# Key rows of a cached window turned in 32 by 32 blocks on VectorE, with query columns spread by key quarter

## The chip, the core and the metric

The kernel runs on one core of a Trainium2 chip. The metric is the device time of one execution in microseconds (us); where several executions are given, their median counts. TensorE multiplies, VectorE, ScalarE and GpSimd (POOL) work on the two on-chip memories SBUF and PSUM, and SyncE (SP) issues most of the transfers. Each engine runs its own instructions in order and waits on semaphores for the others.

## The reference, cut to what matters

One layer of a decoder: attention and a short gated convolution side by side, one output projection, then a mixture of experts and a gated input embedding. There are 1024 new prompt positions and 8 sample batches of 4 new tokens. The part that the change touches is the samples' attention: each batch has 2048 cached key and value rows of 8 heads by 64, and its 4 tokens see three dilation patterns of them and the batch's own new tokens.

```
DILATED_PATTERNS = ((128, 1), (512, 4), (2048, 16))
s = einsum('bthc,btkhc->bthk', q, kg) * HEAD_DIM ** -0.5 + bias
s = where(valid, s, NEG)
p = softmax(s, axis=-1)
out = einsum('bthk,btkhc->bthc', p, vg)
```

The convolution group computes `B * conv3(C * h)` over 512 channels for all tokens.

## The kernel before

The stages follow each other: projections of q, k and v for all tokens, attention of the prompt (32 steps), then a **convolution stage** that also does the whole sample attention, then the output projection, routing, the experts and the embedding. The last three hold most of the time and are not touched.

The convolution stage makes 12 groups (`NCONV`) of 7 products (`PRODUCTS`), each four f32 matmuls of 128 x 128 by 264 columns; the seven are a fast scheme for a 2 x 2 block product. I call each of these 84 products with what hangs behind it a **slot**. The product of a slot goes to one of three PSUM banks in turn. ScalarE copies the first four of a group (`keep_product`), VectorE adds the seven together in "joins" (`join_product`), multiplies the gates (`use_first`, `use_second`) and makes the three taps of the convolution (`taps`), and POOL prepares sums of the next group's weights. A product may start when its bank has been read.

The sample attention is cut into parts (`SAMPLE_PARTS`), and `spread_parts` gives each part a slot in proportion to its `ROOM`. In its slot every engine does its own share of the part, after the product or its joins: on VectorE, before, ahead of the taps. The parts of batch b:

- ("key", b, gg), gg = 0 to 3: the 896 cached rows that the patterns need (512 near, 384 far) lie in a ring slot `KV` of three. For two heads (128 columns) TensorE turns the seven 128 x 128 blocks (`keys`, L2816 and L2820), and ScalarE copies the two banks to `near` and `far` (L1387, L1391).
- ("score", b): TensorE multiplies the keys with the query columns `qbd`, for 512, 384 and 32 (new) columns, four heads' pairs at a time on four strips of the array (`score_keys`, L2837). Four batches share one score bank pair.
- "soft", "norm" and ("turn", g) follow once for each **pass** g of four batches: VectorE adds the bias and finds the maximum (L2077), ScalarE takes the exponential, VectorE divides (L2082), TensorE turns the weights in eight blocks (`turn_ps`) and ScalarE copies them to `PTs`.
- ("weigh", b) multiplies the weights with the values (`weigh_values`), VectorE masks the result by head (L2090), and ("sum", b) adds the rows that belong together (L2877).

SP loads the ring: four transfers per item, when the item three places earlier has been used up; between them stand the loads of the convolution's weights, in the order of their slots. At the start SP also loads small tables, among them eight transfers of the bias table into `relbd` (L707), ahead of the first saves of turned rows (`keep_xT`, L717).

## Time and profile before

| what | value |
| --- | --- |
| median of 3 runs | 1082.56 us (1079.72 to 1084.94) |
| the profiled execution | 1082.67 us |
| its span, first to last instruction | 1080.7 us |
| granted TensorE clock, mean | 0.982 of full speed |
| TensorE busy | 1036.0 us, 96% |
| VectorE busy | 523.0 us, 48% |
| ScalarE busy | 312.7 us, 29% |
| convolution stage | 280.13 to 498.25 us |

A busy share is an average over stages. The profile can also be cut into windows, into groups of instructions by line, or listed in order of time; beside an instruction it says how long its engine idled before it and what ended that. Times of single instructions overlap a little at their ends.

### The profile page before, as it was taken

The page shows a single profiled execution, that of the slowest core. Times are in us where ns is not written, and L with a number is a line of the kernel's source. Part 1 is how long each engine was busy: PE and PEld are TensorE (multiplying, and loading weights), DVE is VectorE, ACT ScalarE, POOL GpSimd, SP SyncE. Part 2 cuts the span into 40 slices and gives each one's busy share as a digit, 9 for nine tenths or more (in the row PEclk, how much of TensorE's full clock was granted, in tenths as well). Part 3 has the DMA queues.
Part 4 walks back from the last instruction along what each step waited for, and adds up shares of the span by engine and source line. Part 5 has one row for each costly group of instructions (what it writes and reads, how often), then busy time and mean ns, then how long its engine had stood idle before and what let it go on. Part 6 is the DMA issues. An engine that isn't in the chain of part 4 may idle for free.

```text
span 1080.7 us, 15684 instructions
## 1 busy us (share of the span) xinstructions
PE 1036.0 (96%) x5834; PEld 620.1 (57%) x5834; DVE 523.0 (48%) x1175; ACT 312.7 (29%) x665; POOL 212.4 (20%) x240
## 2 busy tenths in 40 slices
PE   7999999999999999999999999989999999889997
PEld 6888875565878777766555554334433333345443
DVE  6836634777733464545556464441111110047674
ACT  2332313777533322301111123111111111244331
POOL 0100001121433352531012111322231110130000
PEclk9999999999999999999999998989999999989999
DMA  9713214940563666663973237989999999974321
GB/s 315 190 31 116 71 50 119 293 101 6 215 213 112 212 211 216 207 244 81 355 270 128 94 105 280 405 340 414 418 410 410 419 420 399 371 288 157 119 78 78
DMA packets 99260, 242.11 MB, mean 224 GB/s; under 512 B 21206, under 2 KB 56958, under 8 KB 84528
## 3 DMA queue, kind: packets, MB, share of 16 engines
q1 hardware_dynamic: 88544, 212.10, 54.1%
q0 software_dynamic: 9920, 26.38, 6.4%
q10 hardware_dynamic: 720, 2.62, 0.6%
q8 instruction: 48, 0.79, 0.3%
q14 instruction: 28, 0.23, 0.1%
HBM read 210.12 MB, written 35.65 MB: 227 GB/s over the span
## 4 chain that ended last, share of the span: by engine, by line
PE 80%; DVE 6%; DMA 6%; SPq 4%; issue 2%; ACT 2%; POOL 0%; POOLq 0%; DVEq 0%; ACTq 0%
PE pair L2921 13%; PE pair L3124 13%; PE pair L2598 10%; PE pair L2976 9%; PE pair L3146 6%; PE pair L3228 5%; PE pair L3223 3%; PE pair L2739 2%; DMA h_dram<-R 2%; DMA R<-in_w_up 2%; PE pair L2713 2%; PE pair L3047 2%; PE pair L2755 2%; PE pair L3111 1%; SPq L707 1%
## 5 line engine op out<-in xcount | busy, mean ns | idle before, releaser
L2921 PE MATMUL pair<-R 128*128 128x264 f32 x672 | 160.2, 389 | 0.2 <-POOL R L1032 0.2
L3124 PE MATMUL pair<-R 128*32 128x512 f32 (+2 forms) x896 | 151.3, 601 | 5.2 <-DMA R<-in_w_up 3.0
L2598 PE MATMUL pair<-R 128*128 128x256 f32 x672 | 149.7, 382 | 0.4 <-DVE R L1755 0.4
L2598 PEld LDWEIGHTS pair<-R 128*128 128x128 f32 x672 | 127.0, 191 | 18.8 <-issue 1.0
L2921 PEld LDWEIGHTS pair<-R 128*128 128x128 f32 x672 | 123.5, 190 | 23.4 <-issue 3.5
L2976 PE MATMUL pair<-R 128*128 128x512 f32 x256 | 116.6, 606 | 0.0
L2329 DVE TENSOR_TENSOR R<-pair,R 128x256 f32<-128x256 f32 x21 | 8.9, 425 | 208.3 <-ACT R L1516 208.3
L3124 PEld LDWEIGHTS pair<-R 128*32 128x32 f32 (+2 forms) x896 | 48.8, 125 | 92.2 <-issue 87.8
L3146 PE MATMUL pair<-R,bias 128*32 128x512 f32 (+2 forms) x448 | 78.0, 611 | 2.7 <-issue 2.1
L2976 PEld LDWEIGHTS pair<-R 128*128 128x128 f32 x256 | 47.7, 192 | 53.3 <-issue 52.6
L3228 PE MATMUL pair<-R 128*128 128x512 f32 x168 | 73.0, 593 | 0.0
L1031 POOL TENSOR_TENSOR R<-R 128x256 f32<-128x256 f32 x48 | 38.2, 796 | 115.8 <-DMA R<-in_w_in 113.6
L1953 DVE TENSOR_TENSOR R<-R 128x264 f32<-128x264 f32 x48 | 29.7, 619 | 56.2 <-ACT R L1371 55.2
L3228 PEld LDWEIGHTS pair<-R 128*128 128x128 f32 x168 | 31.5, 190 | 38.2 <-issue 38.2
L1371 ACT ACTIVATE R<-pair 128x264 f32<-128x264 f32 x48 | 18.8, 391 | 107.7 <-PE pair L2921 107.7
L1516 ACT ACTIVATE R<-pair 128x256 f32<-128x256 f32 x21 | 8.1, 384 | 137.5 <-PE pair L3124 137.5
L3146 PEld LDWEIGHTS pair<-R,bias 128*32 128x32 f32 (+2 forms) x448 | 23.4, 125 | 41.9 <-issue 39.5
L1127 POOL DMA_INDIRECT R<-m_dram,lists x21 | 21.3, 1013 | 122.9 <-PE pair L3111 87.9
L1767 DVE TENSOR_TENSOR R<-pair,R 128x256 f32<-128x256 f32 x48 | 20.3, 422 | 44.2 <-PE pair L2598 43.8
L1888 DVE CUSTOM_DVE_ANT_0 R<-pair,R 128x384 f32<-128x384 f32 (+6 forms) x64 | 32.4, 544 | 16.2 <-issue 15.7
L1032 POOL TENSOR_TENSOR R<-R 128x256 f32<-128x256 f32 x48 | 40.2, 838 | 0.0
L1135 POOL DMA_INDIRECT y_dram<-R,lists x21 | 21.0, 1002 | 97.6 <-ACT R L1528 94.3
(366 smaller groups left out, 1471.5 us busy)
## 6 DMA issues: line engine op xcount, KB each, us to landing
R<-in_w_gate SPq DMA_DIRECT2D x32, 1024.0 KB, 12.3
R<-in_w_up SPq DMA_DIRECT2D x32, 1024.0 KB, 15.6
R<-in_w_down SPq DMA_DIRECT2D x32, 1024.0 KB, 16.8
R<-in_w_in SPq DMA_DIRECT2D x12, 1024.0 KB, 8.4
R<-in_x_prompt SPq DMA_DIRECT2D x16, 512.0 KB, 3.8
R<-in_cache_k SPq DMA_DIRECT2D x8, 1024.0 KB, 5.0
R<-in_cache_v SPq DMA_DIRECT2D x8, 1024.0 KB, 4.9
R<-y_dram SPq DMA_DIRECT2D x16, 512.0 KB, 5.9
```

What stands on the lines that cost most here:

```text
L1031: pool.tensor_tensor(out[:, 0:2, :], x[:, 0:2, :], y[:, 0:2, :], op)
L1032: return pool.tensor_tensor(out[:, 2:4, :], x[:, 2:4, :], y[:, 2:4, :], op)
L1888: dve.tensor_tensor_reduce(E[n % 3][hh][:, lo:hi], bk[2 * (n % 2) + hh][:, lo:hi], Z[s][:, at + lo:at + hi], -1.0, 3e38, ALU.add, ALU.min, ...
L1953: dve.tensor_tensor(out, x, y, op).then_inc(S("cv_join"), 1)
L2598: last = mm(qbank(p, part, k), lhs[:, c, :], rhs[:, c, :], start=(c == 0), stop=(c == 3))
L2713: last = mm(dst[hh][:, near_lo:hi], QT[halves_[hh], pair, P * i:P * i + P], KT[halves_[hh], pair, k0:P * i + P], start=True, stop=True)
L2921: last = mm(cbank(n, k), lhs[:, c, :], rhs[:, c, :], start=(c == 0), stop=(c == 3))
L2976: last = mm(bk[2 * pair + j][0:n, :], lhs[:, q, P * a.t:P * a.t + P], w_out[:, c0 + q, 512 * j:512 * j + 512], start=(q == 0), stop=(q == ...
L3124: last = mm(bk[2 + u][r, :].rearrange("p (w f) -> p w f", w=2), xgT[u][:, c, r], wgu[s][:, :, c, :], start=(c == 0), stop=(c == DC - 1))
L3146: last = mm(bk[4 + j][r, :], hT[u][:, q, r], wd[s][:, q, 512 * j:512 * j + 512], start=(q == 0), stop=(q == 1))
L3223: last = mm(bk[2 + j], hnT[i][:, c, :], w_pg[c][:, 512 * j:512 * j + 512], start=(c == 0), stop=(c == DC - 1))
L3228: last = mm(pbank(p, nth), x[:, c, :], w[:, c, :], start=(c == 0), stop=(c == 3))
```

## The change

**Keys.** TensorE no longer turns the keys. A key's near rows are loaded so that the 32 partitions of quarter i hold the rows of one residue (four transfers instead of one; the far rows three as before), and VectorE turns a ring slot's rows in blocks of 32 x 32 straight into `kT` (two instructions per key part, `turn_keys`). Within a partition quarter there now lies a quarter of the rows (224) for 32 of a head's 64 channels. So a batch's scores are 16 matmuls of 256 columns (224 cached, 32 new), and the query columns are spread such that each key quarter meets its own copy (`spread_q`, with masks `in_strip`).

**Passes.** A pass is two batches instead of four (`NPASS` = 4). A row of scores now belongs to one key quarter, so the minimum and the sum over a head's four quarters are taken with small block turns (`by_group`). The weights' turn is four matmuls against a permuted identity, four times instead of twice, and six ScalarE copies behind each.

**Order.** `SAMPLE_PARTS` is written by `sample_order`; soft and norm have places of their own; the ring's items alternate between keys and values earlier. In a slot VectorE now does the taps ahead of the sample part.

**Elsewhere.** The sample's q and k are turned by 32 small matmuls (`trans_qk`) in place of eight turns, and VectorE copies q to `q4` in 16 copies inside the attention steps 9 to 24. The eight loads of `relbd` have a quarter of their former elements and stand behind the first two `keep_xT`; VectorE completes the table with one copy. The bias is added by quarter.

```diff
-SAMPLE_PARTS = (("key", 0, 0), ("key", 0, 1), ("key", 0, 2), ("key", 0, 3), ("score", 0),
...
-ROOM = {"key": 4, "score": 4, "turn": 6, "weigh": 8, "sum": 4}
+def sample_order():
+    parts = []
+    for g in range(NPASS + 1):
+        keys = [[("key", 2 * g + d, gg) for gg in range(NG)] if g < NPASS else [] for d in range(2)]
+        if g == 0:
+            parts += keys[0] + [("score", 0)] + keys[1] + [("score", 1), ("soft", 0)]
+            continue
+        b = 2 * g - 2
+        parts += [*keys[0][0:1], ("norm", g - 1), *keys[0][1:2], ("turn", g - 1), *keys[0][2:4]]
+        if g < NPASS:
+            parts += [("score", 2 * g)]
+        parts += [("weigh", b), *keys[1][0:2], ("sum", b), ("weigh", b + 1), *keys[1][2:4]]
+        if g < NPASS:
+            parts += [("score", 2 * g + 1), ("soft", g)]
+        parts += [("sum", b + 1)]
+    return parts
+ROOM = {"key": 4, "score": 6, "soft": 2, "norm": 2, "turn": 4, "weigh": 8, "sum": 4}
...
+        def turn_keys(b, gg):
+            slot, arrived = item("k", b)
+            kv = KV[slot]
+            if gg == 0:
+                dve.wait_ge(S(f"ring_in{slot}"), arrived)
+                if b >= 1:
+                    dve.wait_ge(S("ss_done"), b)
+                else:
+                    dve.wait_ge(S("ssa_full"), 1)
+            raw = kv[:, :, P * gg:P * gg + P].rearrange("p c (n x) -> p c n x", n=4)
+            out = kT[:, 4 * gg:4 * gg + 4, 0:PART].rearrange("p n (c r) -> p c n r", c=7)
+            dve.transpose(out[:, 0:4], raw[:, 0:4])
+            dve.transpose(out[:, 4:7], raw[:, 4:7]).then_inc(S("kt_done"), 1)
...
         def score_sample(g):
-            dve.wait_ge(S("ss_done"), 4 * g + 4)
-            if g == 1:
-                dve.wait_ge(S("st_full"), 3)
-            dve.tensor_tensor_reduce(Es, bank[3][:, 0:SKN], bias_s[:, :], -1.0, 3e38, ALU.add, ALU.min, nms).then_inc(S("ss_scored"), 1)
+            dve.wait_ge(S("ss_done"), 2 * g + 2)
+            if g >= 1:
+                dve.wait_ge(S("st_full"), g)
+            for s in range(2):
+                then(dve.tensor_tensor_reduce(Es[:, s, :], bk[6 + g % 2][:, ROW * s:ROW * s + ROW], bias_s, -1.0, 3e38, ALU.add, ALU.min,
+                                              least[:, s:s + 1]))
+                if 2 * g + s + 1 < NB:
+                    new_bias(2 * g + s + 1)
+            by_group(least_t, ALU.min, least, group_least, nms).then_inc(S("ss_scored"), 1)
+            for b in (2 * g + 2, 2 * g + 3):
+                if b < NB:
+                    spread_q(b)
...
         def normalise_sample(g):
-            dve.wait_ge(S("ss_exp"), g + 1)
-            then(dve.reciprocal(rdens, dens))
-            dve.tensor_scalar(Es, Es, rdens, None, ALU.mult).then_inc(S("ps_ready"), 1)
+            dve.wait_ge(S("ss_exp"), 2 * g + 2)
+            then(by_group(dens_t, ALU.add, dens, group_den, rdens))
+            for s in range(2):
+                dve.tensor_scalar(Es[:, s, :], Es[:, s, :], rdens[:, s:s + 1], None, ALU.mult).then_inc(S("ps_ready"), 1)
...
+                if n >= 1 and k < 3:
+                    taps(n - 1, k)
                 for part in PARTS_AT.get(at, ()):
                     sample_part(*part)
-                if n >= 1 and k < 3:
-                    taps(n - 1, k)
...
         def score_keys(b):
-            for c0, c1, rhs in ((0, NEAR, near), (NEAR, SK, far), (SK, SKN, kts)):
-                for gg in range(NG):
-                    last = mm(bank[3][strips[gg], c0:c1], qbd[:, bb, gg, :], rhs[:, gg, :],
+            pe.wait_ge(S("kt_done"), NG * b + NG)
+            pe.wait_ge(S("qbd"), 16 + b + 1)
...
+            for hh in range(2):
+                for half in range(2):
+                    for j in range(NG):
+                        n = 4 * j + 2 * hh + half
+                        at = 32 * n + (0 if hh else 16)
+                        last = mm(out[strips[j], ROW * second:ROW * second + ROW], qbd_all[second][:, at:at + 32], kT[:, n, :],
...
         def turn_ps(g):
+            by_quarter = ident[:, :].rearrange("p (g i t) -> p i g t", g=H, i=4)
+            pe.wait_ge(S("ps_ready"), 2 * g + 2)
...
+            for c in range(4):
+                last = mm(bk[4][:, P * c:P * c + P], Es[:, c // 2, P * (c % 2):P * (c % 2) + P], by_quarter, start=True, stop=True)
```

The slots that result, for the parts that others wait for: scores of batches 0 to 7 in slots 8, 13, 21, 31, 40, 51, 59 and 70 (before: 9, 15, 21, 28, 36, 45, 54, 63); each batch's fourth key part one slot earlier; soft in 15, 33, 52 and 71, norm in 16, 35, 55 and 73, turn in 18, 37, 56 and 73.

TensorE, the convolution stage from the second key part of batch 0 to the product behind its scores, before (L2921 a product of four matmuls, L2816 and L2820 a key part, L2837 the scores):

```order
L2921 MATMUL pair<-R 128x264 x4
L2816 MATMUL pair<-ident,R 128x128 x4
L2820 MATMUL pair<-ident,R 128x128 x3
L2921 MATMUL pair<-R 128x264 x4
L2816 MATMUL pair<-ident,R 128x128 x4
L2820 MATMUL pair<-ident,R 128x128 x3
L2921 MATMUL pair<-R 128x264 x8
L2837 MATMUL pair<-R 32x512 x4
L2837 MATMUL pair<-R 32x384 x4
L2837 MATMUL pair<-kts,R 32x32 x4
L2921 MATMUL pair<-R 128x264 x4
```

and now (first the squares that stand ahead of slot 4, L2955 the products, L2880 the scores, L2890 the weights' turn):

```order
L2921 MATMUL pair<-ones,R 128x1 x8
L2955 MATMUL pair<-R 128x264 x20
L2880 MATMUL pair<-R 32x256 x16
L2955 MATMUL pair<-R 128x264 x20
L2880 MATMUL pair<-R 32x256 x16
L2955 MATMUL pair<-R 128x264 x20
L2890 MATMUL pair<-ident,R 128x128 x4
L2955 MATMUL pair<-R 128x264 x12
L2880 MATMUL pair<-R 32x256 x16
L2955 MATMUL pair<-R 128x264 x4
```

The key turns are gone, twenty matmuls (five products) stand in one run ahead of each of the first scores, and the first turn of weights stands three products ahead of the third batch's scores.

VectorE, slots 38 and 39, before (L1953 joins, L1935, L1940 and L1942 sums for the second span of the convolution, L2090 the mask of batch 0's values):

```order
L1953 TENSOR_TENSOR R<-R 128x264 [waits cv_join,cv_kept]
L1953 TENSOR_TENSOR R<-R 128x264 [waits cv_join]
L1935 TENSOR_TENSOR R<-R 128x1056
L2090 TENSOR_TENSOR R<-pair,R 128x512 [waits small_in,so_full]
L1953 TENSOR_TENSOR R<-pair,R 128x264 [waits cv_join,cv_full]
L1953 TENSOR_TENSOR R<-R 128x264 [waits cv_join]
L1968 TENSOR_TENSOR R<-R 128x264 [waits conv,cv_join]
L1969 TENSOR_TENSOR R<-R 128x264
L1940 TENSOR_TENSOR R<-R 128x1056 [waits cv_full,cv_t]
L1953 TENSOR_TENSOR R<-pair,R 128x264 [waits cv_join,cv_full]
L1942 TENSOR_TENSOR R<-R 128x4x264
L1953 TENSOR_TENSOR R<-R,pair 128x264 [waits cv_join,cv_full]
```

and now (L1979 joins, L1961 and L1966 the sums, L2107 and L2108 a key part of batch 4):

```order
L1979 TENSOR_TENSOR R<-R 128x264 [waits cv_join,cv_kept]
L1979 TENSOR_TENSOR R<-R 128x264 [waits cv_join]
L1961 TENSOR_TENSOR R<-R 128x1056
L2107 STREAM_TRANSPOSE R<-R 128x4x4x32
L2108 STREAM_TRANSPOSE R<-R 128x3x4x32
L1979 TENSOR_TENSOR R<-pair,R 128x264 [waits cv_join,cv_full]
L1979 TENSOR_TENSOR R<-R 128x264 [waits cv_join]
L1994 TENSOR_TENSOR R<-R 128x264 [waits conv,cv_join]
L1995 TENSOR_TENSOR R<-R 128x264
L1966 TENSOR_TENSOR R<-R 128x1056 [waits cv_full,cv_t]
L2107 STREAM_TRANSPOSE R<-R 128x4x4x32
L2108 STREAM_TRANSPOSE R<-R 128x3x4x32
```

Two key parts stand in these slots, each behind the joins and the sum; the mask no longer stands there.

VectorE, the first softmax, before (L2077 scores plus bias, L2066 query columns, L2081 and L2082 the division, L2004 taps):

```order
L2077 ISA R,small<-pair,bias 128x928 [waits ss_done]
L2077 ISA small 128x1
L2066 COPY R<-qts 64x4x4 [waits ss_done]
L2066 COPY R<-qts 64x4x4 x7
L2071 COPY bias<-bias 128x32 [waits ss_scored]
L2019 COPY R<-R 128x2 [waits conv,cv_used,r_step]
L2020 TENSOR_SCALAR R<-R,convw 128x528
L1953 TENSOR_TENSOR R<-R 128x264 [waits cv_join,cv_kept]
L2081 RECIPROCAL small<-small 128x1 [waits ss_exp]
L2082 TENSOR_SCALAR R<-R,small 128x928 [waits r_step]
L2004 SCALAR_TENSOR_TENSOR R<-R,convw 128x528 [waits conv] x2
L1953 TENSOR_TENSOR R<-R 128x264 [waits cv_join,cv_kept]
```

and now, from slot 15 (L2030 a tap, L2123 scores plus bias, L2111 to L2115 the steps over quarters, L2086 the query columns):

```order
L2030 SCALAR_TENSOR_TENSOR R<-R,convw 128x528 [waits conv]
L2123 ISA R<-pair,bias 128x256 [waits ss_done]
L2123 ISA R 128x1
L2094 COPY bias<-bias 128x32 [waits r_step]
L2123 ISA R<-pair,bias 128x256 [waits r_step]
L2123 ISA R 128x1
L2094 COPY bias<-bias 128x32 [waits r_step]
L2111 STREAM_TRANSPOSE R<-R 128x32 [waits r_step]
L2112 TENSOR_REDUCE R<-R 128x8 [waits r_step]
L2115 STREAM_TRANSPOSE R<-R 128x32 [waits r_step]
L2086 TENSOR_TENSOR R<-bias,misc 128x16x16 x2
L2107 STREAM_TRANSPOSE R<-R 128x4x4x32 [waits ss_done,ring_in2]
```

The one pass over 928 columns has become two over 256 with small steps between them that wait for each other (`r_step`), the next batch's first key part follows, and the division comes behind that.

## Rows read from the trace of the kernel before

**Rows 1.** the page's busy line: engine, busy us, share, instructions.
```profile
PE 1036.0 (96%) x5834; PEld 620.1 (57%) x5834; DVE 523.0 (48%) x1175; ACT 312.7 (29%) x665; POOL 212.4 (20%) x240
```

**Rows 2.** by windows: length, busy us of each engine, clock, DMA share, GB/s.
```profile
192.00:280.13 88.13, 84.36 (x941) 53.84 (x941) 67.86 (x225) 66.42 (x181) 15.61 (x19) 0.98 0.40 111
280.13:498.25 218.12, 217.02 (x1313) 168.87 (x1314) 113.63 (x232) 60.88 (x132) 84.67 (x100) 1.00 0.61 210
```

**Rows 3.** groups by line, 280 to 498 us: busy us, mean ns, idle before.
```profile
L2816 PE MATMUL pair<-ident,R 128*128 128x128 f32 x128 | 19.2, 273 | 0.0
...
L1371 ACT ACTIVATE R<-pair 128x264 f32<-128x264 f32 x48 | 18.8, 391 | 107.7 <-PE pair L2921 107.7
...
L2820 PE MATMUL pair<-ident,R 128*128 128x128 f32 x96 | 15.7, 273 | 0.0
...
L2877 PE MATMUL pair<-R 128*128 128x4 f32 x64 | 8.3, 253 | 0.9 <-ACT R L1409 0.9
...
L2837 PE MATMUL pair<-kts,R 128*32 128x32 f32 x64 | 2.0, 194 | 0.0
```

**Rows 4.** in order of time, TensorE: start us, us, line, tiles, shapes.
```profile
309.04 0.60 PE L2816 MATMUL pair<-ident,R 128*128 128x128 f32 x4
...
311.59 0.60 PE L2816 MATMUL pair<-ident,R 128*128 128x128 f32 x4
...
312.35 3.73 PE L2921 MATMUL pair<-R 128*128 128x264 f32 x16
315.92 0.60 PE L2816 MATMUL pair<-ident,R 128*128 128x128 f32 x4
...
318.56 1.71 PE L2837 MATMUL pair<-R 128*32 128x512 f32 x16
...
320.26 2.05 PE L2921 MATMUL pair<-R 128*128 128x264 f32 x8
```

**Rows 5.** in order of time, VectorE, from four stretches.
```profile
38.80 1.22 DVE L1712 TENSOR_REDUCE small<-R 128x16 f32<-128x1024 f32 x1 [1.09 <-ACT R L1242]
...
220.76 1.80 DVE L1899 TENSOR_SCALAR R<-R,small 128x416 f32<-128x416 f32 x2
...
353.47 1.12 DVE L2077 CUSTOM_DVE_ANT_0 R<-pair,bias 128x928 f32<-128x928 f32 x1 [2.88 <-PE pair L2837]
...
357.36 0.70 DVE L2082 TENSOR_SCALAR R<-R,small 128x928 f32<-128x928 f32 x1
...
372.24 0.43 DVE L1953 TENSOR_TENSOR R<-R 128x264 f32<-128x264 f32 x1 [3.36 <-ACT R L1371]
372.59 1.57 DVE L2004 SCALAR_TENSOR_TENSOR R<-R,convw 128x528 f32<-128x528 f32 x2
...
384.46 1.25 DVE L1940 TENSOR_TENSOR R<-R 128x1056 f32<-128x1056 f32 x1
...
649.25 0.19 DVE L2222 TENSOR_REDUCE R<-R 128x1 f32<-128x32 f32 x1
```

**Rows 6.** in order of time, TensorE, in the expert stage.
```profile
711.31 0.70 PE L3133 MATMUL pair<-ident,R 128*128 128x128 f32 x2 [2.69 <-DVE R L2329]
712.51 9.86 PE L3124 MATMUL pair<-R 128*64 128x512 f32 x32 [0.49 <-DVE R L2324]
```

**Rows 7.** by windows, the same place.
```profile
712.00:716.00 4.00, 3.51 (x11) 1.03 (x12) 0.45 (x1) 0.38 (x1) 0.00 (x0) 0.50 1.02 384
```

**Rows 8.** the chain that ended last, the same form at another place.
```profile
750.64 7.02 PE pair L3124 x32
```

**Rows 9.** in order of time, TensorE, attention: the sample's q.
```profile
199.48 0.43 PE L2629 MATMUL pair<-ident,R 32*128 32x32 f32 x4
```

**Rows 10.** waits, 190 to 282 us: total, times, longest.
```profile
PE pair L2739 <- DVE R L1899: 5.0, 7, 1.6
```

**Rows 11.** in order of time, SP's queue, the start.
```profile
20.85 14.16 SPq L707 DMA_DIRECT2D R<-in_rel_bias  x8
```

**Rows 12.** in order of time, TensorE, the start.
```profile
46.76 1.13 PE L2585 MATMUL pair<-ident,R 128*128 128x128 f32 x8 [0.83 <-DVE R L1704]
```

More of the change, by code:

```diff
@@ L67 @@
 SKN = SK + SAMP
+NPASS = NB // 2
+PART = SK // 4
+ROW = PART + SAMP
 CAP = 128
@@ L224, with place_of @@
 PARTS_AT = spread_parts()
-def place_of(kind, b, gg=None):
-    return next(s for s, parts in PARTS_AT.items() for part in parts if part[0:2] == (kind, b) and (gg is None or part[2] == gg))
+def place_of(part):
+    return next(s for s, parts in PARTS_AT.items() if part in parts)
 NSTAT = 6
@@ L2096, in sample_part @@
         def sample_part(kind, b, *more):
[L2097 to L2098 removed]
+            if kind == "key":
+                turn_keys(b, more[0])
+            if kind == "soft":
+                score_sample(b)
+            if kind == "norm":
+                normalise_sample(b)
             if kind == "weigh":
                 mask_sample(b)
[L2101 to L2105 removed]
             if kind == "sum":
                 keep_sum(b)
[L2108 to L2109 removed]
         dve.wait_ge(S("late_in"), 16 * NLATE)
@@ L2867, in weigh_values @@
             for k in range(FARC):
-                mm(bk[3][strips[k], :], rows(4 + k, P), KV[slot][:, 4 + k, :], start=False, stop=True)
-            last = mm(bk[3][strips[3], :], rows(7, P), V[:, PT, :], start=False, stop=True)
+                mm(bk[3][strips[k], :], PTs[:, second, 1, k, :], KV[slot][:, 4 + k, :], start=False, stop=True)
+            last = mm(bk[3][strips[3], :], PTs[:, second, 1, 3, :], V[:, PT, :], start=False, stop=True)
             last.then_inc(S("so_full"), 1)
```

337 lines of the change are left out of this document (156 added, 181 removed).

## The prediction

> **What bounds the kernel now.** I read the page's busy line first, then the table by stage, then inside one stage the groups by line, the waits and the rows in order of time. TensorE is busy 96% of the span [rows 1]; in the convolution stage, 280.13 to 498.25 us, it is busy 217.02 of 218.12 us, VectorE 113.63 and ScalarE 60.88 [rows 2]: it idles 1.1 us. So this stage lasts as long as the sum of TensorE's instructions, and VectorE does its part beside them. The reader is to see one more thing in those numbers: VectorE is not idle but half full, and it is the engine on which the change puts work.
>
> I call "slot" one of the 84 convolution products with what the table of parts hangs behind it. Two slots of which one has a key part start at 311.59 and 315.92, one with a key part takes 309.04 to 311.59 = 2.55 us; so a bare product takes 4.33 - 2.55 = 1.78 us and a key part 0.77 us on TensorE's path [rows 4], although its seven turns add up to (19.2 + 15.7) / 32 = 1.09 us of busy time [rows 3]: they overlap the products at both ends, and 0.77 is what can be won.
>
> **What goes from TensorE.** 32 key parts x 0.77 = 24.6 us, and with them 64 ScalarE copies that nobody waited for.
>
> **What TensorE gets.** A batch's scores are now 16 matmuls of 256 columns, four at a time on four strips (1024 column steps) instead of 928 steps. Before, they take 318.56 to 320.26 = 1.70 [rows 4]; 1.70 x 1024/928 is 0.2 more, x 8 = 1.6. The weights' turn is four full matmuls (two records each) instead of eight transposes, and four times instead of twice. A matmul that loads 128 x 128 weights for few columns costs 8.3 / 32 = 0.26 us [rows 3]; four are 1.1, four passes 4.4; the old ones, 16 turns of the size of the key turns at 0.77 / 7 each, 1.8. That is +2.6. Net on TensorE: -24.6 + 1.6 + 2.6 = **-20.4 us**, if nobody is late. Weighing and summing of values keep their matmuls.
>
> **What VectorE gets.** A key part is two block turns of 512 and 384 elements per partition. No row shows this operation. A one-source pass over 1024 elements takes 1.22 us, one over 32 takes 0.19 [rows 5], so 1.04 ns per element: 0.69 + 0.56, less 0.08 that each instruction starts ahead of the last one's end (372.24 + 0.43 against 372.59 [rows 5]): **1.12 us**. Below: the scaling of 928 elements in 0.70 us [rows 5] gives 0.57 ns per element, 0.70 us a part. Above: two scalings of 416 elements took 1.80 us where POOL works on the same memory [rows 5], 2.2 ns per element, 1.9 us. I take 1.12, the one-source pass being the nearest kin. 32 parts are 36 us in a stage where VectorE has 100 us free, so the mean fits; the question is the place. Each small step of the softmax costs 0.22 with its wait (0.19 [rows 5]). "Soft" is two scorings of 256 (0.42 each, scaled from 1.12 for 928 [rows 5] by the same 1.04 ns), a small copy behind each and three small steps, 1.9 us, then two spreads of 0.42: 2.8; "norm" four steps and two scalings of 0.32: 1.5.
>
> **Where it stands on the path.** TensorE's scores wait until VectorE has turned a batch's fourth part, one slot earlier; its weights' turn waits for soft, exp and norm, at most three slots earlier. Behind TensorE's wait stand all products. VectorE in turn takes the joins of each product first, and may begin those of a kept product only 0.46 us after its end (the copy's 391 ns [rows 3], then the join). Join 0.43, tap 0.79, both [rows 5]. So:
> - Scores of batch 3: the parts stand behind taps in two slots: 0.46 + 0.43 + 0.79 + 1.12 + 0.79 + 1.12 = 4.7, against two products less their tail, 3.4: wait 1.3. Batch 6 the same with longer taps 1.6; batch 5 has one such slot, 1.3; batch 7 0.5.
> - Batch 4: its last two parts share their slots with two sums for the second span, 1.25 each [rows 5], and with the y products: 0.46 + 0.86 + 1.25 + 1.12 + 0.86 + 1.3 + 1.24 + 1.12 = 8.2 against 3.4: wait 4.5 (a little overlap taken off).
> - Batch 0: VectorE enters late from its memsets as before; four parts in a row and 3.4 of joins end some 2.4 after TensorE arrives. Batch 1 inherits it, 1.3.
> - Turn 0: 0.46 + 0.43 + 0.79 + 2.8 + 1.12 + 0.79 + 1.5 = 7.9 against three products, 5.2: 2.7. Batch 2's scores, 8.8 of queued work against a turn and three products, 6.4: 2.4.
> - Turn 1 0.2, turn 2 2.0, by the same count with their own joins. Turn 3: ScalarE's exps stand ahead of the copies that the joins need, and the joins ahead of norm, 8.3 against 4.3: 4.0.
>
> The sum is **24.2 us**; all cover that the 20.4 needed is gone. A wait also lowers the clock. Ahead of 711.31 TensorE idles 2.69 us [rows 6]; then the granted clock is 0.50, the 1.2 GHz level [rows 7], and 32 records take 9.86 us [rows 6] that take 7.02 elsewhere [rows 8]: 2.8 us. Three of my waits are as long (2.7, 4.5, 4.0): 8.5, of which I take half, since VectorE catches up in that time: +4.2.
>
> **Elsewhere.** Attention: the sample's q and k are turned by 32 matmuls on strips; 64 records of that size cost 2.0 us [rows 3], four turns before 0.43 [rows 9], eight 0.8: +1.2. Sixteen VectorE copies of about 0.2 there; that stage has waits of TensorE on VectorE of 5.0 us in all [rows 10], so a quarter counts: +0.8 (0 to 3.2). Start: the eight small loads hold SP's queue from 20.85 for 14.16 us [rows 11], and behind them the save of rows for which VectorE and then TensorE wait, TensorE 0.83 [rows 12]; they now come behind that save: -0.8, what TensorE idles there and no more. SP issues seven key transfers per batch instead of four, three per value batch; a queued weight load may slip 2 us in one place where VectorE is late anyway: 0 to 2, taken 0.
>
> **Sum.** -20.4 + 24.2 + 4.2 + 1.2 + 0.8 - 0.8 = +9.2. The profiled run is 1082.67 us (span 1080.7), the median of the three 1082.56, the same: **1092 us**, its own range 1086 to 1101.
>
> **Rivals.**
> - *The cover holds (faster).* The turn costs 0.70 a part, and the small steps of soft and norm mostly overlap: the batches' waits shrink by the two to four parts in their chains, the turns' by half, some 10 us are left and no wait is long enough for the clock: 1082.7 - 20.4 + 10 + 1.2 = 1073. It decides from waits under 14 us. For it: 100 us of VectorE's stage are free. Against: the batch 4 and turn 3 chains, 7 us together by joins and sums alone.
> - *It cancels.* Turn at 0.70, softmax as I have it: waits 15, one half-clock stretch of 2.8: 1081.
> - *The block turn is slow.* A price of 1.9 or more, POOL's sums beside it: each of the eight batch waits grows by 1.6, each turn by 0.8, the clock by three more stretches: 1092 + 13 + 3 + 8 = 1116.
>
> The Trainium skill speaks against the change: "VectorE: DVE Perf Modes", section "Rules for kernel authors", leaves full 128 x 128 turns to TensorE where PSUM will do, and its section "The three transpose paths" has 311 ns for such a turn on VectorE against 390 on TensorE (bf16). An estimate by that: seven blocks are 2.2 us a part, which is the slow rival's side; TensorE's seven cost 0.77 on the path here [rows 4], far less than the page's 390 each, so by row and page together the exchange is a poor one unless VectorE's time is free. No run so far shows the VectorE number.
>
> **Chances.** Forecast 0.46, cancels 0.24, cover holds 0.22, slow turn 0.08. A measurement of this kernel tells 0.5% (5.4 us) from no change. Faster 0.24 (the cover rival and the low edge of the cancelling one), same 0.25 (the rest of it and the forecast's low edge), slower 0.51. The range leaves out the slow rival and a tenth at the fast end: 1070 to 1107.
>
> **What would show it.** In the stage by windows: TensorE's busy time near 197 us; VectorE's near 165. Between 300 and 480 us, waits of TensorE's score and turn lines on VectorE, twelve of them, the longest at batch 4 and turn 3, and a granted clock under 1.0 behind those. A block turn row with 0.6 to 0.7 us for 512 elements. Wrong would be: scores that start right behind their product; a row of 0.45 or of 1.0 for 512; TensorE waiting on the weight sums or on cache loads instead.

## The result, and the profile after

| | median | profiled span | convolution stage |
| --- | --- | --- | --- |
| before | 1083.64 us | 1080.7 us | 280.13 to 498.25, 218 us |
| after | 1236.04 us (1233.65 to 1239.67) | 1235.1 us | 281.90 to 654.07, 372 us |

The ratio is 1.1416 (95% interval 1.1373 to 1.146): 152 us slower. The predicted 1092 us, range 1070 to 1107, had the direction and missed the size. The whole difference lies in the convolution stage: behind it the changed kernel takes 581.0 us, the kernel before 582.5; ahead of it the difference is under 2 us.

After, by windows (length, busy us and count of TensorE, its weight loads, VectorE, ScalarE, POOL, then granted clock, the mean busy share of the core's 16 DMA engines, which the view puts a little over 1 in places, and the GB/s that they moved): the stage, and its first 50 us. They are to be set beside [rows 2].

```profile
281.90:654.07 372.17, 224.21 (x1169) 164.14 (x1170) 145.37 (x346) 35.10 (x98) 78.87 (x100) 0.79 0.47 122
281.90:332.00 50.10, 34.02 (x188) 25.95 (x192) 30.28 (x60) 5.30 (x11) 10.15 (x13) 0.85 0.26 95
```

TensorE idles 148 us of the stage where it had idled 1.1, and VectorE is busy only 145 of 372. No engine became the bound. The last two columns of the second row point to what did: three ring slots of keys are loading and, but for two small tables, nothing else is, yet the DMA engines are busy a quarter of the time and move 95 GB/s.

After, the stage's waits that matter (engine, line, releaser: total us, times, longest):

```profile
POOL R L1057 <- DMA R<-in_w_in: 273.8, 10, 52.9
PE pair L2955 <- POOL R L1058: 106.8, 7, 26.4
PE pair L2880 <- DVE R L2108: 17.3, 6, 8.2
```

The products (L2955) wait 106.8 us for POOL's weight sums, and POOL waits for the weights to arrive. The wait that I had forecast, scores (L2880) for VectorE's turns, is the third row. Why the weights are late stands on SP's queue, in order of time (start us, us, line, transfer, count), after:

```profile
281.87 2.78 SPq L786 DMA_DIRECT2D R<-in_cache_k  x4
284.69 8.05 SPq L788 DMA_DIRECT2D R<-in_cache_k  x3
292.79 10.19 SPq L786 DMA_DIRECT2D R<-in_cache_k  x4
...
321.56 6.21 SPq L788 DMA_DIRECT2D R<-in_cache_k  x3
...
332.99 0.64 SPq L770 DMA_DIRECT2D R<-in_w_in  x1
```

and before:

```profile
285.70 1.90 SPq L768 DMA_DIRECT2D R<-in_cache_k  x3
...
296.14 0.57 SPq L753 DMA_DIRECT2D R<-in_w_in  x1
```

The first four key transfers go out in 2.78 us; from then on one of 256 KB holds SP's queue for some 2.5 us instead of 0.6. So the third group's weights go out at 332.99 instead of 296.14. SP also stands for another reason, a wait of its own in the stage, after:

```profile
SPq L790 <- DVE R L2108: 82.4, 5, 29.7
```

A value load waits there until VectorE has turned the keys in its buffer, and weight loads stand behind it; e9 and e10 come back to this. POOL starts its sums at 346.52, after, in order of time (the bracket is its idle time and what ended it):

```profile
346.52 0.72 POOL L1057 TENSOR_TENSOR R<-R 128x256 f32<-128x256 f32 x1 [52.91 <-DMA R<-in_w_in]
```

and TensorE its next product at 351.03, the same view:

```profile
351.03 10.74 PE L2955 MATMUL pair<-R 128*128 128x264 f32 x40 [18.13 <-POOL R L1058]
```

There are seven such waits in the stage (19.25, 26.40 and 24.89 us among the others). Behind such a wait the granted clock is low: 0.50 from 455.60 to 460.00 us, behind the one of 26.40. Over the stage it is 0.79, against 1.00 before.

The block turns themselves, groups by line (busy us, mean ns | idle before):

```profile
L2107 DVE STREAM_TRANSPOSE R<-R 128x512 f32<-128x512 f32 x32 | 22.5, 704 | 17.1 <-DMA R<-in_cache_k 17.1
L2108 DVE STREAM_TRANSPOSE R<-R 128x384 f32<-128x384 f32 x32 | 17.1, 535 | 0.0
```

### The profile page after: what moved, and what is told of

It is laid out like the page before. It is cut to its first block, busy times and chain, and to the rows that moved or that the text cites. A ratio compares the mean times of both kernels' runs of the same rounds, so it can differ in the third digit from the quotient of the medians.

```text
span 1235.1 us, 15551 instructions
## 1 busy us (share of the span) xinstructions
PE 1041.8 (84%) x5750; PEld 616.9 (50%) x5750; DVE 558.6 (45%) x1308; ACT 286.8 (23%) x631; POOL 205.1 (17%) x240
## 4 chain that ended last, share of the span: by engine, by line
PE 64%; issue 17%; DVE 6%; DMA 6%; POOL 3%; ACT 2%; SPq 1%; POOLq 0%; DVEq 0%; ACTq 0%
PE pair L2660 12%; PE pair L3158 11%; PE pair L3010 7%; PE pair L2955 6%; PE pair L3180 5%; PE pair L3262 4%; PE pair L3257 2%; PE pair L2808 2%; DMA h_dram<-R 2%; DMA R<-in_w_up 1%; PE pair L3081 1%; PE pair L2824 1%; PE pair L2782 1%; POOL R L1057 1%; PE pair L3145 1%
## 5 line engine op out<-in xcount | busy, mean ns | idle before, releaser
L2955 PE MATMUL pair<-R 128*128 128x264 f32 x672 | 176.1, 421 | 114.0 <-POOL R L1058 106.8
L2955 PEld LDWEIGHTS pair<-R 128*128 128x128 f32 x672 | 136.3, 208 | 152.9 <-issue 121.9
L2660 PEld LDWEIGHTS pair<-R 128*128 128x128 f32 x672 | 127.4, 192 | 18.2 <-issue 0.6
L1979 DVE TENSOR_TENSOR R<-R 128x264 f32<-128x264 f32 x48 | 22.6, 471 | 160.4 <-ACT R L1397 159.5
L1057 POOL TENSOR_TENSOR R<-R 128x256 f32<-128x256 f32 x48 | 36.0, 750 | 276.7 <-DMA R<-in_w_in 274.9
L3010 PEld LDWEIGHTS pair<-R 128*128 128x128 f32 x256 | 47.1, 190 | 52.9 <-issue 51.5
L3262 PEld LDWEIGHTS pair<-R 128*128 128x128 f32 x168 | 31.5, 190 | 38.2 <-issue 38.2
L1788 DVE TENSOR_TENSOR R<-pair,R 128x256 f32<-128x256 f32 x48 | 20.3, 422 | 43.7 <-PE pair L2660 43.4
L1344 ACT ACTIVATE R<-R,small 128x384 f32<-128x384 f32 (+6 forms) x64 | 38.3, 606 | 0.0
```

Of the source, the lines that this page charges most:

```text
L1057: pool.tensor_tensor(out[:, 0:2, :], x[:, 0:2, :], y[:, 0:2, :], op)
L1344: act.activation(E[n % 3][hh][:, lo:hi], E[n % 3][hh][:, lo:hi], ACT.Exp, bias=nmax[:, k:k + 1], scale=-1.0, accum_out=den[:, k:k + 1]).th ...
L1979: dve.tensor_tensor(out, x, y, op).then_inc(S("cv_join"), 1)
L2660: last = mm(qbank(p, part, k), lhs[:, c, :], rhs[:, c, :], start=(c == 0), stop=(c == 3))
L2955: last = mm(cbank(n, k), lhs[:, c, :], rhs[:, c, :], start=(c == 0), stop=(c == 3))
L3010: last = mm(bk[2 * pair + j][0:n, :], lhs[:, q, P * a.t:P * a.t + P], w_out[:, c0 + q, 512 * j:512 * j + 512], start=(q == 0), stop=(q == ...
```

## What the experiments asked

Theory A: a transfer whose outermost dimension is 4 is carried by a quarter of the DMA engines. In the changed kernel a key's near rows are read as [4 residues][32 rows][512], the far rows as [4][32][512], the near values as [4][32][2048], the far ones as [3][32][1536]; before, every one had 32 or 128 outermost. Rivals: the number and size of the pieces (B), the ring's new order (C), VectorE (D).

| run | what it is | median us | ratio to before (95%) |
| --- | --- | --- | --- |
| e1_quarters | changed, loads split by partition quarter | 1121.18 | 1.0373 (1.0335 to 1.0411) |
| e2_keys | only its keys split | 1185.26 | 1.095 (1.0914 to 1.0986) |
| e3_values | only its values split | 1203.20 | 1.1116 (1.1081 to 1.115) |
| e4_whole | changed, rows renumbered, loads over 96 or 128 partitions but for the far keys | 1107.77 | 1.0234 (1.019 to 1.0277) |
| e5_order | e4, sample part ahead of the taps | 1104.72 | 1.0191 (1.0149 to 1.0233) |
| e6_noturn | e4, hardly any turns on VectorE | 1093.18 | 1.0105 (1.0053 to 1.0158) |
| e7_far4 | before, far loads with 4 outermost | 1138.63 | 1.0528 (1.0496 to 1.0559) |
| e8_split | before, near loads in four | 1087.75 | 1.0041 (1.0022 to 1.006) |
| e9_slack | e4, scores one part later | 1111.99 | 1.0265 (1.0228 to 1.0302) |
| e10_room | e9 and e5, weight loads first in SP's order | 1087.34 | 1.0037 (1.0023 to 1.0051) |
| e11_plain | e10, turn without a stride, near values into 32 partitions each | 1086.40 | 1.0018 (0.9994 to 1.0041) |
| e12_turn | e10, weights' turn later, more room for some parts | 1073.76 | 0.9904 (0.9886 to 0.9922) |

## The outermost dimension: e1 to e3, e7

**e1**, the key loads (the values likewise, by chunk; here and below, dots mark lines left out, and some semaphore calls are left out at the ends of lines):

```diff
-for c in range(4):
-    sp.dma_start(kv[:, c, :], near_rows[c])
-for k in range(FARC):
-    sp.dma_start(kv[:, 4 + k, :], ck[b][512 * k:512 * k + 512, :].rearrange("(r a) d -> a r d", a=16)[0:4])
...
+for i4 in range(4):
+    sp.dma_start(kv[32 * i4:32 * i4 + 32, 0:4, :], near_rows[i4])   # [32 r][4 c][512]
+    sp.dma_start(kv[32 * i4:32 * i4 + 32, 4:7, :], far_rows[i4])    # [32 r][3 k][512]
```

> The changed kernel with every cache load split by partition quarter, so that the outermost dimension of each transfer is 32 rows instead of 4 or 3: eight transfers for a batch's keys instead of seven, eight for its values instead of three; same rows to the same places. Theory A (a transfer whose outermost dimension is 4 is carried by a quarter of the DMA engines; SP's queue and the weight loads behind it are late for that): DMA share while the caches load goes from 0.25 to over 0.8, the landing of a weight load from 18 to about 8 us, the convolution stage from 372 to about 227 us, the kernel to 1080 to 1105 us. Rival B (it is the number and size of the pieces, 896 of 2 KB for a batch's keys): as many pieces remain, so 1220 to 1240. Rival C (the ring's order makes loads wait for VectorE's turns, whatever their speed): over 1180, with SP waiting on the turns. Rival D (VectorE's work is the bound): over 1150, TensorE's waits then name VectorE.

> As the first, but only the key loads are split by quarter; the value loads stay with outermost dimensions 4 and 3. Per batch 1.75 MB of keys then load fast and 1.56 MB of values (outermost 4 and 3) at about 100 GB/s or less, some 16 us each, 130 us for eight batches. Theory A: between the two, 1110 to 1160 us, the value transfers alone showing a DMA share near 0.25. Rival B: no gain, 1220 to 1240.

> As the first, but only the value loads are split; the key loads keep their outermost dimension of 4 (1.75 MB a batch at about 100 GB/s, 18 us each, 145 us for eight). Theory A: 1130 to 1190 us, the key transfers alone showing a DMA share near 0.25. Rival B: no gain, 1220 to 1240.

e1 measured 1121.18, 115 us less than the changed kernel, with the same rows in the same places and more transfers (eight instead of seven for a batch's keys, eight instead of three for its values). By their own figures B, C and D had no room for that: as many 2 KB pieces, the same ring, the same work on VectorE. But it stayed 16 us above the top of A's own figure, and TensorE still waits for POOL's sums:

```profile
PE pair L2957 <- POOL R L1060: 20.4, 6, 6.4
```

Its windows, the stage and 10 us of key loads:

```profile
281.00:534.25 253.25, 210.54 (x1169) 156.84 (x1167) 152.09 (x346) 35.16 (x98) 81.95 (x100) 0.94 0.79 179
290.00:300.00 10.00, 8.18 (x38) 6.69 (x37) 9.66 (x20) 0.69 (x2) 2.56 (x4) 1.00 1.06 206
```

All DMA engines now work (share about 1), yet the rate is 206 GB/s, where the kernel before has 386 at the same share (its row stands with e8). So A does not account for all of it; e4 and e8 take that up. e2 (1185.26) and e3 (1203.20) missed their ranges upwards: they win 51 and 33 us, together 84 of the 115. The weight loads queue behind whichever kind is still slow, so half a cure is less than half the gain.

**e7** measures the dimension by itself, in the kernel before, where nothing else of the change is present:

```diff
-row[NEAR:] = 512 * (col // P) + 16 * (col % P // NT) + col % NT
+row[NEAR:] = 512 * (col // P) + 16 * (col % 32) + col % P // 32
-src[b][512 * k:512 * k + 512, :].rearrange("(p a) d -> p a d", a=16)[:, 0:NT, :]
+src[b][512 * k:512 * k + 512, :].rearrange("(r a) d -> a r d", a=16)[0:NT]
```

> The kernel before, its far loads alone changed: the same 48 transfers of 128 pieces of 2 KB, and the rows renumbered so that the source's outermost dimension is 4 (four runs of 32 rows) instead of 32 (runs of four rows). Nothing else moves. Theory A (a transfer with an outermost dimension of 4 is carried by a quarter of the DMA engines): the 48 transfers go at about 100 GB/s, 2.6 us each one after the other, 126 us of the stage's 218; SP's hold on an issue goes from 0.60 to some 2.5 us where they queue; a weight load behind three of them is some 8 us late. TensorE's stage then waits where the loads are tight: 1085 to 1125 us. Rival B (pieces and their number): unchanged, 1080 to 1086, landing 5 to 6 us.

1138.63: 55 us from one reordering of 48 transfers, as many, as large, in pieces of the same size (the expected top was 1125). From 290 to 292 us, when TensorE stands, the DMA share is 0.26 at 89 GB/s. The order in which the rows are read changes with the dimension; it is this share, a quarter, that speaks for the number of engines. The first ones on SP's queue, in order of time:

```profile
281.31 2.06 SPq L765 DMA_DIRECT2D R<-in_cache_k  x1
283.42 9.77 SPq L768 DMA_DIRECT2D R<-in_cache_k  x3
```

9.77 us for three where the kernel before has 1.90, and TensorE waits for the same as in the changed kernel (waits of the stage: total, times, longest):

```profile
PE pair L2921 <- POOL R L1032: 34.9, 6, 10.9
PE pair L2816 <- DMA R<-in_cache_k: 4.9, 1, 4.9
```

The Trainium skill has the rule, in "DMA: Bandwidth & Descriptors", section "Why a DMA increments its semaphore by 16 and not by 1" and again in its "Rules for kernel authors": the number of engines, at most 16, is the largest that divides the slowest dimension of both patterns, so 4 rows outermost mean 4 engines. The share of 0.26 at 95 GB/s in the changed kernel agrees. I had not weighed that rule when I predicted.

## Thirty-two partitions: e4 and e8

**e4** renumbers the rows so that a near load of keys is again one transfer of 128 x 8 KB and one of values is [128][4][512]; the far keys stay split by quarter:

```diff
...
-first = np.where(chunk < 4, PAST - NEAR + 16 * r + 4 * chunk, 512 * (chunk - 4) + 16 * r)
...
+first = np.where(chunk < 4, PAST - NEAR + 4 * r + chunk, 512 * (chunk - 4) + 16 * r)
+step = np.where(chunk < 4, 128, 1)
...
+sp.dma_start(kv[:, 0:4, :].rearrange("p c d -> p (c d)"),
+             ck[b][PAST - NEAR:PAST, :].rearrange("(p c) d -> p (c d)", c=4)).then_inc(arrived, 16)
...
+sp.dma_start(kv[:, 0:4, :], cv[b][PAST - NEAR:PAST, :].rearrange("(i p) d -> p i d", i=4)).then_inc(arrived, 16)
...
-dve.transpose(out[:, 0:4], raw[:, 0:4])
+dve.transpose(kT[:, 4 * gg:4 * gg + 4, 0:P].rearrange("p n (r c) -> p c n r", c=4), raw[:, 0:4])
```

> The changed kernel with rows renumbered so that a transfer reaches 96 or 128 partitions: a batch's near keys one transfer of 128 x 8 KB as in the kernel before, its near values one of 128 partitions (4 pieces of 2 KB each), its far values one of 96 partitions and one of 32; only the far keys stay split by quarter (four of 192 KB). The first turn of a key part writes its 512 elements with a stride of four. Theory A2 (beside the outermost dimension, a transfer into only 32 partitions is held to about 210 GB/s, the split kernel's rate at a full DMA share): the rate while the caches load returns to 300 to 430 GB/s, a weight load lands in about 8 to 9 us, TensorE's 20 us of waits for POOL's weight sums go, its 20 us for VectorE stay: 1088 to 1103 us. Rival B2 (the number of 2 KB pieces): 20% fewer than in the split kernel, 1110 to 1122. Rival C2 (the order of the ring holds the weight loads back, whatever the transfers' rate): 1110 to 1122, with SP waiting on turns of VectorE ahead of weight loads. If the strided write is slow, the first turn of a part shows well over 0.70 us, and VectorE's waits grow.

1107.77, 13 us below e1, but 5 above the range of A2 and 2 below that of its rivals. TensorE waits 4.0 us for POOL instead of 20.4, as A2 had it, and VectorE does more, as the last case of the expectation had it. But a weight load lands in 10.5 us (median in the stage; e1: 11.4), not in 8 to 9. The gain over e1 has three candidates that e4 does not separate: partitions, fewer transfers and fewer 2 KB pieces. The waits of TensorE in its stage:

```profile
PE pair L2957 <- POOL R L1060: 4.0, 3, 1.7
PE pair L2882 <- DVE R L2110: 20.3, 8, 5.5
PE pair L2892 <- DVE R L2138: 8.6, 3, 3.2
```

The strided write takes 1.10 us instead of 0.70, by its group:

```profile
L2109 DVE STREAM_TRANSPOSE R<-R 128x512 f32<-128x512 f32 x32 | 35.0, 1095 | 0.3 <-PE pair L2882 0.3
```

**e8**, in the kernel before, sets a load into 32 partitions against one into 128 with the same 256 KB:

```diff
+for j in range(4):
+    part = (slice(32 * j, 32 * j + 32), slice(0, 4)) if kind == "k" else (slice(0, P), slice(j, j + 1))
+    sp.dma_start(kv[:, 0:4, :][part[0], part[1], :].rearrange("p a d -> p (a d)"),
+                 near_rows[part[0], part[1], :].rearrange("p a d -> p (a d)")).then_inc(S(f"ring_in{i % 3}"), 16)
```

> The kernel before, its near load of 1 MB in four transfers of 256 KB: for a batch's keys by partition quarter (32 partitions, 8 KB each), for its values by row (128 partitions, 2 KB each). Same bytes, and the outermost dimension is 32 or more in both. Theory A2 (32 partitions alone take about 210 GB/s): keys' four transfers last some 5 us together, landing of the last 7 to 9 us, the values' four some 2.7 us, landing 4 to 6; the kernel within 0.5% of before, as the stage's loads have room: 1079 to 1089. If pieces of 2 KB are what is slow: the values' transfers are the slow ones. If neither: both land alike, and the renumbered kernel's gain over the split one came from the number of transfers.

The time is 0.4% up, within the expected span. From issue to landing a key transfer takes 6.0 us (median in the stage), a value transfer 4.4. The windows: two stretches of mostly near key loads, one of near value loads, and one with the last of the values and a weight load behind them:

```profile
283.00:287.00 4.00, 4.00 (x20) 3.42 (x19) 3.56 (x7) 0.79 (x2) 4.00 (x6) 1.00 0.96 219
320.00:324.00 4.00, 4.00 (x38) 2.73 (x31) 2.85 (x3) 0.67 (x2) 1.94 (x3) 1.00 0.92 204
336.00:338.00 2.00, 2.00 (x28) 1.18 (x19) 0.00 (x0) 0.45 (x1) 0.00 (x0) 1.00 0.88 264
340.00:342.00 2.00, 2.00 (x14) 1.76 (x13) 0.07 (x1) 1.01 (x3) 0.00 (x0) 1.00 0.99 335
```

Before, with a batch's key loads, near in one transfer and far in three:

```profile
319.00:323.00 4.00, 4.00 (x40) 2.95 (x33) 2.39 (x3) 0.59 (x3) 2.42 (x3) 1.00 1.03 386
```

At a DMA share near 1, the transfers by partition quarter go at 204 to 219 GB/s although their pieces are 8 KB; the values' 2 KB pieces over 128 partitions go at 264 at a share of 0.88, and from 325 to 326 us, when by the order of issue only a batch's far keys are left (pieces of 2 KB over 128 partitions), the rate is 344. So pieces of 2 KB are not what makes the quarters slow. Both kinds are four transfers here, so their number alone is not it either; whether it costs the values something, 264 being less than 386, is open. The Trainium skill, "SBUF — State Buffer", section "Door 1: The DMA port swizzle", says that partitions 0 to 31 reach 8 of 16 ports, 218 GB/s at most; the rows agree with the number, and nothing here looks at ports themselves.

## VectorE's waits and the order: e5, e6, e9 to e12

With the loads mended, e4's TensorE shows eleven of the twelve waits of the prediction, each ahead of a score (L2882) or a weights' turn (L2892). In order of time, the first four, then batch 4 and the last turn:

```profile
303.81 1.93 PE L2882 MATMUL pair<-R 128*32 128x256 f32 x32 [2.78 <-DVE R L2110]
...
317.11 1.93 PE L2882 MATMUL pair<-R 128*32 128x256 f32 x32 [2.27 <-DVE R L2110]
...
331.12 1.16 PE L2892 MATMUL pair<-ident,R 128*128 128x128 f32 x8 [2.98 <-DVE R L2138]
...
340.72 3.21 PE L2882 MATMUL pair<-R 128*32 128x256 f32 x32 [3.10 <-DVE R L2110]
...
395.55 3.64 PE L2882 MATMUL pair<-R 128*32 128x256 f32 x32 [5.50 <-DVE R L2110]
...
494.02 2.07 PE L2892 MATMUL pair<-ident,R 128*128 128x128 f32 x8 [3.17 <-DVE R L2138]
```

| wait | scores 0 | 1 | 2 | 3 | 4 | 5 | 6 | 7 | turn 0 | 1 | 2 | 3 | sum |
| --- | --- | --- | --- | --- | --- | --- | --- | --- | --- | --- | --- | --- | --- |
| predicted | 2.4 | 1.3 | 2.4 | 1.3 | 4.5 | 1.3 | 1.6 | 0.5 | 2.7 | 0.2 | 2.0 | 4.0 | 24.2 |
| e4 | 2.8 | 2.3 | 3.1 | 1.5 | 5.5 | 1.4 | 3.5 | under 0.5 | 3.0 | under 0.5 | 2.4 | 3.2 | 28.9 |

**e5** is e4 with the sample part again ahead of the taps:

```diff
-if n >= 1 and k < 3:
-    taps(n - 1, k)
 for part in PARTS_AT.get(at, ()):
     sample_part(*part)
+if n >= 1 and k < 3:
+    taps(n - 1, k)
```

> As the kernel with renumbered rows, but in VectorE's program the sample part stands again ahead of the taps (one part of the change undone). If the taps ahead of the parts are what makes TensorE's scores late (the prediction counted 0.79 us in two or three places of most waits): 4 to 10 us less than the kernel with renumbered rows. If the softmax and the joins of the next products set the waits: within 3 us of it. If the taps are then late for the y products: slower by 2 to 6 us.

1104.72 against 1107.77: the intervals overlap, and the waits for VectorE are 26.6 us instead of 28.9. So this shows at most a small gain: the order of taps and part is not the main cost of the change.

**e6** leaves out most turns from batch 1 on:

```diff
+if b >= 1:
+    dve.transpose(out[:, 4:5, 0:1], raw[:, 4:5, 0:1]).then_inc(S("kt_done"), 1)
+    return
```

> As the kernel with renumbered rows, but from the second batch on a key part turns only one block of 32 by 32 per partition strip instead of 28 (part of the computation left out): VectorE loses some 27 us, TensorE's program is the same. If the turns are what TensorE's scores wait for: nearly all waits for the turns go, and the kernel falls by 12 to 25 us, to 1068 to 1080; this is then also the most that the removal of the 32 TensorE turns could bring (20.4 predicted, less the softmax's waits). If the waits come from the softmax, the weights' turn or the loads: within 5 us of the kernel with renumbered rows.

1093.18: 14.6 us less, as forecast, but from e4's higher level, so not 1068 to 1080. The scores' waits fall from 20.3 to 7.5 us; the weights' turns still wait 6.7 and POOL's sums 5.7. So without most of the turns e4 is still 1% slower than the kernel before: 14.2 us of waits for the rest of VectorE's work stay, 2.8 of them at batch 0, whose turns are still made.

**e9** puts a part between a batch's last key part and its scores:

```diff
-parts += [*keys[0][0:1], ("norm", g - 1), *keys[0][1:2], ("turn", g - 1), *keys[0][2:4]]
+parts += [*keys[0][0:1], ("norm", g - 1), *keys[0][1:2], ("turn", g - 1), *keys[0][2:4], ("weigh", b)]
...
-parts += [("weigh", b), *keys[1][0:2], ("sum", b), ("weigh", b + 1), *keys[1][2:4]]
+parts += [*keys[1][0:1], ("sum", b), *keys[1][1:4], ("weigh", b + 1)]
```

> As the kernel with renumbered rows, but a batch's scores come one part later: the weighing of an earlier batch (two slots) now stands between its last key part and its scores, for batches 2 to 7; the second batch's key parts and sum close up by that. If TensorE waits because VectorE's queue has peaks one slot ahead of the scores (my count in the prediction): six of the eight waits for the turns shrink from 2.9 us each to under 1, TensorE's waits for VectorE go from 29 to some 15 us, the kernel 8 to 16 us less, 1092 to 1100. If VectorE is late by its sum of work: the waits move to the next parts, 1103 to 1112.

The scores' waits go as expected, 20.3 to 6.5 us, and the kernel gets no faster (1111.99): POOL's waits come back, in the list of the stage's waits.

```profile
PE pair L2957 <- POOL R L1060: 17.4, 3, 10.1
PE pair L2892 <- DVE R L2138: 10.1, 3, 4.7
PE pair L2882 <- DVE R L2110: 6.5, 3, 3.2
```

The same list for SP's own queue has the reason:

```profile
SPq L793 <- DVE R L2110: 88.2, 7, 20.9
```

SP stands 88 us at value loads, whose buffer is free when VectorE has turned the keys in it; the weight loads queue behind. This stand is not new: e4 has 90.4 us of it, and the changed kernel the 82.4 shown above. With the parts moved, weights that TensorE soon needs stand behind it again: one goes out at 402.88, behind a stand that ended at 398.31 and the loads of a value and a key item, and POOL has it at 417.67.

**e10** takes e9 and e5 and moves the weight loads ahead; **e11** takes the turn without a stride, with near values in four transfers of 32 partitions:

```diff
-return place_of(("key", b, NG - 1)) if kind == "k" else place_of(("weigh", b))
+return 4 + (place_of(("key", b, NG - 1)) if kind == "k" else place_of(("weigh", b)))
```

> Renumbered rows, scores one part later, sample part ahead of the taps, and on SP's queue a weight load goes ahead of a cache load whose buffer comes free up to four slots before the weight load's own (with the later scores TensorE waited 17 us for POOL's weight sums, 10.1 us at once, behind an SP queue that stood 88 us for VectorE's turns). If that queue order is the cause of those waits: POOL's waits under 4 us, VectorE's stay at some 15, the kernel 1090 to 1098 us. If POOL is late for another reason: 1105 to 1112.

> The same, but the turn writes without a stride (0.70 us instead of 1.10 for 512 elements, 12.6 us less of VectorE's time), for which the near values load in four transfers of 32 partitions again (about 205 GB/s). If VectorE's time is worth more than that rate: 2 to 8 us below its neighbour. If the slow transfers hold back weight loads again: above it, with POOL's waits over 8 us.

e10 is 1087.34, 25 us below e9 and below its range. TensorE's waits in the stage are now these, with none for POOL:

```profile
PE pair L2892 <- DVE R L2138: 10.1, 3, 4.4
PE pair L2882 <- DVE R L2110: 5.5, 3, 2.3
```

SP stands 28.6 us at the value loads instead of 88.2, and a weight load lands in 6.0 us (median) instead of 10.7. So SP's order was the cause of POOL's waits. e5's order is in e10 too and was not run without it; on e4 it left POOL's waits as they were (4.2 us against 4.0). e11, 1086.40, is the same within the intervals: 9.5 us less of VectorE's busy time in the stage (154.74 against 164.26) buy nothing measurable, and one wait for POOL of 4.7 us is back. What remains in e10 are the weights' turns, 10.1 us, and scores, most of it at the first two batches.

**e12** gives those room:

```diff
-*keys[0][1:2], ("turn", g - 1), *keys[0][2:4], ("weigh", b)
+*keys[0][1:3], ("turn", g - 1), *keys[0][3:4], ("weigh", b)
+def room(part):
+    return ROOM[part[0]] + (4 if part in (("key", 0, 3), ("key", 1, 3)) else 6 if part == ("norm", NPASS - 1) else 0)
```

> As the kernel with renumbered rows, later scores, the sample part ahead of the taps and weight loads first, with room for the two kinds of wait that are left there (weights' turn 10.1 us in three waits of 3.4, 2.4 and 4.4; scores of the first two batches 2.3 each): the weights' turn stands one key part later, the last norm gets a slot and a half more, and the first two batches' scores a slot more. If a wait is a matter of the order alone: TensorE's waits for VectorE fall from 15.6 to under 7 us, the half-clock stretches behind them go, and the kernel is at 1074 to 1081 us, faster than before by 0.2 to 0.8%: the predicted gain of TensorE's work is then real and was hidden by the waits. If VectorE is late by the sum of its work: the waits move to scores or joins, 1084 to 1090 us.

1073.76: 1.0% faster than before, where 0.2 to 0.8% was expected, and at the low edge of its range, 0.24 us under it. The stage by windows:

```profile
280.00:489.25 209.25, 199.40 (x1168) 151.53 (x1169) 166.90 (x346) 35.51 (x98) 89.13 (x100) 0.98 0.76 216
```

and its scores' waits for the turns:

```profile
PE pair L2887 <- DVE R L2115: 5.1, 3, 2.1
```

The weights' turns wait once, 2.36 us at 332.05. That is 7.5 us in all, where e10 has 15.6 and under 7 was expected. TensorE is busy 199.40 us against 217.02 [rows 2], VectorE 166.90 against 113.63: the same turns as in e4 (161.92), in a stage 30 us shorter.

## Why the prediction was wrong

- **What bounds the kernel** (TensorE's sum, VectorE half free): right for the kernel before, and again in e12, where the stage is 209.25 us with TensorE busy in 199.40. In the changed kernel it is not: TensorE is busy 224.21 of 372.17 us and waits for weights.
- **The step that failed** is the sentence on the loads: "a queued weight load may slip 2 us in one place where VectorE is late anyway: 0 to 2, taken 0". I counted transfers, seven for four, and had no row for what one in the new form costs. The price was not a matter of the count: in the new form one holds the queue 2.5 us instead of 0.6, and the first weight load slipped 36.9 us. e1 puts 115 of the 152 us on the outermost dimension. e4 wins a further 13, net of its slower turns; e8's rates speak for the loads into 32 partitions, but no run separates them from e4's smaller number of transfers. SP's stand for VectorE's turns, 82.4 us in the changed kernel, was not in the sum either. With fast loads its reordering is worth up to 25 us (e9 to e10); what it would be worth in the change as it stands was not run. "TensorE waiting on the weight sums" stood in the prediction as a sign of being wrong, but without a chance or a price. The direction came out right, but not for the reason given: the waits for VectorE that I had forecast are 17.3 us at the scores and 5.3 at the turns in the changed kernel, a small part of 152.
- **TensorE's net, -20.4**: right. A batch's scores stand 1.87 us on the path in e4 (368.61 to the next product at 370.48) against 1.9; the weights' turn 0.89 (383.65 to 384.54) against 1.1. That makes -24.6 + 1.4 + 1.8 = -21.4. e12's busy time is 17.6 under before's, with its half-clock pieces still in it.
- **VectorE's key part, 1.12 us**: right. Two turns of 704 and 535 ns; with the overlap a part takes 303.97 to 305.06 = 1.09 us in the rows below. The prediction's own sum does not give its 1.12: 0.69 + 0.56 less 0.08 is 1.17, and less 0.08 for each of the two turns 1.09. The slow-turn rival falls, and with it the estimate of 2.2 us from the page "VectorE: DVE Perf Modes" of the Trainium skill: four 128-column turns of f32 take 704 ns here, 176 each, against its 311 in bf16. That figure is for 32 x 32 blocks, as the turns here are, and not for the full turn that the prediction made of it; the rule that it held against the change is on full turns too.
- **The twelve waits, 24.2 us**: right in place, and as far as the runs can tell nearly in size. e4 has 28.9 in eleven places, with a part of 1.5 us; e1, whose part is the predicted one, has 20.3 (13.9 and 6.4), some of them perhaps hidden behind POOL's 20.4. No run has both fast loads and the plain turn in the change's own order, so what that would give is open; I would expect it at or under e4's 1108.
- **Half clock, +4.2**: right in size, in four places instead of three. In e4 the scores of batches 2 and 4 take 3.21 and 3.64 us instead of 1.93, two turns 2.07 instead of 1.16: 1.3 + 1.7 + 0.9 + 0.9 = 4.8.
- **Elsewhere**: the sample's q takes 0.75 us where [rows 9] had 0.43, so q and k +0.6 (predicted +1.2); waits of that stage on VectorE 5.9 against 5.0 in [rows 10], +0.9 (predicted +0.8); the 0.83 us at the start [rows 12] are gone, -0.8 as predicted. Not foreseen: 1.8 us for VectorE's sums at the stage's start.
- **The rivals.** None had the price of the loads in it: 1236 lies above the dearest, 1116. By e4's rows the sum, made against the span, is 1080.7 - 21.4 + 28.9 + 4.0 + 4.8 + 1.8 + 0.7 = 1099.5, against a span of 1103.4; 3.9 us stay unexplained. "The cover holds", 1073, came true only in e12, after the order had been written for it, and that 1073.76 stands so close to it is luck: a part takes 1.5 us there, not the rival's 0.70. The cover was there on average, as that rival had it, and not at the places where TensorE asked.

After, VectorE in order of time, a key part and the join behind it:

```profile
303.97 0.71 DVE L2107 STREAM_TRANSPOSE R<-R 128x512 f32<-128x512 f32 x1 [6.47 <-DMA R<-in_cache_k]
304.61 0.54 DVE L2108 STREAM_TRANSPOSE R<-R 128x384 f32<-128x384 f32 x1
305.06 0.39 DVE L1979 TENSOR_TENSOR R<-pair,R 128x264 f32<-128x264 f32 x1
```

After, TensorE in order of time, at the start (no idle time is noted now) and the sample's q in attention:

```profile
47.13 5.35 PE L2660 MATMUL pair<-R 128*128 128x256 f32 x24
...
199.77 0.75 PE L2698 MATMUL pair<-ident,R 32*32 32x32 f32 x64
```

After, the attention stage's wait that answers [rows 10]:

```profile
PE pair L2808 <- DVE R L1920: 5.9, 9, 1.6
```

## What to carry to other kernels

When a change rewrites an access pattern of a transfer, read the outermost dimension on both sides and the partitions that it reaches before counting transfers: loads of the same bytes went at 95, 204 or 386 GB/s. An in-order queue passes a slow transfer's price on to whatever stands behind it, here weights that had nothing to do with the change, so look there for the wait. And where work moves to an engine that is half free, the mean says nothing about the end: consumers need a part's distance from their producers, and the queues that feed them must be reordered with them, or the wait only moves (e9).

## What the runs showed of the hardware

- A load with 4 outermost: DMA share 0.26, 95 GB/s, 2.5 us of SP's queue for 256 KB, against 0.6 us before. The first four such transfers go out in 2.78 us, the next seven in 8.05 and 10.19, so the price shows as issue time once several are in flight.
- A load into 32 partitions: 204 to 219 GB/s at a DMA share near 1; into 128 partitions, 264 (share 0.88) and 344 in two loads with 2 KB pieces, and 386 in the mix before.
- A block turn of 512 f32 per partition: 704 ns; the same with its output written at a stride of four elements: 1095 ns.
